# Expert results scattered to rows of token and choice, tokens gathered in quarter rows ahead and turned on VectorE

## The chip, the cores and the metric

The kernel runs on one core of a Trainium2 chip. The metric is the device time of one execution in microseconds. The kernel before took 2192.16 us, the median of 3 runs (2192.0 to 2193.31 us).

## What is computed

A decoder layer on 1024 tokens of width 1024: a token mixer (a state space model, a gated unit and a cross attention, merged and projected), then a mixture of experts, then a norm. The mixer is not touched by the change. Of the experts this matters:

```
g_idx = argmax(xf @ w_group + b_group)              # one of 8 groups
top_vals, top_loc = top_k(logits of the group's 8 experts, 2)
weights = group probability * softmax(top_vals)     # 2 choices per token
per expert e:  y = (silu(xb @ w1[e]) * (xb @ w3[e])) @ w2[e]
h = h + sum over the 2 choices of weight * y;  out = rmsnorm(h, g_final)
```

There are 64 experts. w1 and w3 are 1024x512 and w2 is 512x1024, all float32, so an expert's weights are 6.29 MB and all of them 403 MB. The 2048 pairs of token and choice are spread unevenly. With the given inputs the reference's routing gives 39 experts of at most 32 tokens, 17 of 33 to 64, 6 of 65 to 96, one of 105 and one of 130.

## The kernel before, in words

All five engines' programs are written out by hand, with semaphores between them. The order is: the mixer; an output stage over 8 tiles of 128 tokens, which also makes the norm of each tile, its router logits and its places in a table of tokens by expert; the expert stage; a last stage over 8 tiles that sums, norms and stores.

**The expert stage.** A unit is up to 32 tokens (`CAP`) of one expert; here there are 100 units. The 64 experts are put in an order that alternates light and heavy ones (`place_col`, L1792 to L1804) and take turns in four slots of SBUF (`SLOTS`), one set of weights each. Every engine runs the same two loops, `each_unit` (L403): over the experts, where it loads three numbers (first unit of the slot, end, shift) from `spans` into registers (L409 to L411), and inside over the units of the expert.

- SyncE (`refill`, L568): when the last unit of the slot's old expert has done its up products, it issues the new expert's token list (L575) and w1 and w3 (L520), and after its down products w2 (L524).
- GpSimd (`gather`, L711): waits until the last gather has landed, copies the unit's column of the list to `gather_idx` (L714), waits until TensorE has turned the last unit's tokens, and issues one indirect DMA of 32 rows of 4 KB into `xg` (L719). `xg` is one buffer.
- TensorE (`work`, L1090): 64 up products from `xT` into a PSUM bank (L1100), the transpose of the hidden rows, then `turn_tokens` (L1083): 8 transposes of the next unit's tokens (both L779), then 32 down products (L1114).
- VectorE: gate times up (L1846), copy of the transposed hidden (L1848), copy of the turned tokens to `xT` (L1841).
- ScalarE (L1319): silu (L1321); then it waits for the stores of the slot's last unit, copies the unit's result to `y_rows` (L1325) and issues four direct DMAs of 32 KB (L1328) to `y_dram`, rows in the order of units.

```
pool.wait_ge(tok_gathered, u * 16 + 16)
nc.gpsimd.tensor_copy(gather_idx[:, :], idx).then_inc(idx_copied, 1)
pool.wait_ge(tok_turned, u + 1)
pool.indirect_dma_start(xg, None, xf_dram, ... gather_idx ...)
```

**The last stage.** After the last stores GpSimd gathers, for each tile of 128 tokens, the rows of both choices from `y_dram` (`pick`, L739, L749), 16 indirect DMAs of 512 KB, into four pairs of buffers (`PICKS`). TensorE sums the even tiles (L772), VectorE the odd ones (L1405, L1879); ScalarE squares, VectorE norms, SyncE stores (L595). The rows of `y_dram` that stand in no unit are cleared early in the mixer by four DMAs of 2 MB (L633).

Of the kernel before, what the change touches and what calls it, by code (L numbers as in the profile page):

```python
# [25 lines left out]
I32 = mybir.dt.int32  # L26
# [32 lines left out]
PICKS = 4  # L59
UNITS = E + 2 * T // CAP  # L60
SLOT_UNITS = TURNS + 2 * T // CAP
# [45 lines left out]
def program(nc, x, mem, g_mix, g_mem, w_in, w_gate, b_gate, lam_re, lam_im, log_dt, b_re, b_im,  # L107
# [3 lines left out]
    with ctx:  # L111
# [37 lines left out]
        token_id = sb("token_id", [P, NT], I32)  # L149
        no_token = sb("no_token", [CAP, 1], I32)  # L150
        table_row = sb("table_row", [P, 2, NT], I32)
        y_row = sb("y_row", [P, 2, NT], I32)
# [3 lines left out]
        spans = sb("spans", [1, 5, E], I32)  # L156
        by_expert = sb("by_expert", [E, 12])
        tokens = sb("tokens", [CAP, SLOTS, COLS], I32)
        gather_idx = sb("gather_idx", [CAP, 1], I32)
# [41 lines left out]
        def tiles(n, k):  # L201
# [28 lines left out]
        pick_rows = unit[9][:, 0:2 * NT * E].rearrange("p (i c e) -> p i c e", i=NT, c=2)  # L230
# [4 lines left out]
        n_units, all_ends = (late[:, 144 + E * n:144 + E * (n + 1)] for n in range(2))  # L235
        pos, base = (late[:, 400 + 16 * n:416 + 16 * n].rearrange("p (i c) -> p i c", i=NT) for n in range(2))
        gsum, den = late[:, 432:440], late[:, 440:448]
        row_of = late[:, 448:464].rearrange("p (i c) -> p i c", i=NT)
# [12 lines left out]
        in_order = now[0:1, 0:5 * E].rearrange("p (n e) -> p n e", n=5)  # L251
# [12 lines left out]
        xg = gain_b[0:CAP, :]  # L264
        xT = gain_a[:, 0:256].rearrange("p (k t) -> p k t", k=KD)
# [5 lines left out]

        y_pick = [[mid_store[:, D * (2 * b + c):D * (2 * b + c + 1)] for c in range(2)] for b in range(PICKS)]
        mix_out = [pair[5][:, D * b:D * (b + 1)] for b in range(PICKS)]
        square_out = pair[5][:, D * PICKS:D * (PICKS + 1)]
        choice_diag = pair[5][:, D * PICKS + D:D * PICKS + 2 * D].rearrange("p (i c t) -> p i c t", i=NT // 2, c=2)
# [6 lines left out]
        table_dram = nc.dram_tensor("expert_token_table", [E * T, 1], I32, kind="Internal").ap()  # L282
        table_of = table_dram.rearrange("(e p n) a -> e p (n a)", e=E, p=CAP)
        y_dram = nc.dram_tensor("unit_results", [UNITS * CAP, D], F32, kind="Internal").ap()
# [7 lines left out]
        x_root, x_row_loaded = sem("x_root"), [sem(f"x_row{i}_loaded") for i in range(NT)]  # L292
# [7 lines left out]
        h_loaded = [sem(f"h_loaded{i}") for i in range(NT)]  # L300
        spatial_loaded, spatial_masked = sem("spatial_loaded"), sem("spatial_masked")
        idx_copied = sem("idx_copied")
        tok_gathered, tok_turned, xT_ready = sem("tok_gathered"), sem("tok_turned"), sem("xT_ready")
# [7 lines left out]
        toep_cleared, results_cleared = sem("toep_cleared"), sem("results_cleared")  # L311
# [6 lines left out]
        table_blank, tile_routed, rows_picked, weighted = (  # L318
            sem("table_blank"), sem("tile_routed"), sem("rows_picked"), sem("weighted"))
        tokens_loaded = [sem(f"tokens_loaded{s}") for s in range(SLOTS)]  # L320
        units_known, order_known = sem("units_known"), sem("order_known")
# [7 lines left out]
        picked = [sem(f"picked{b}") for b in range(PICKS)]  # L329
# [3 lines left out]
        out_stored = [sem(f"out_stored{b}") for b in range(PICKS)]  # L333
# [6 lines left out]
        for family, rows in (  # L340
# [8 lines left out]
                        ("branches", 6 * KD), ("out", 4 * NT), ("order", 2))),  # L349
# [53 lines left out]
        def each_unit(eng, body, enter=None, shift_row=2, less=0):  # L403


            with eng.Fori(0, TURNS) as t:
                for s in range(SLOTS):
                    at = bass.ds(t * SLOTS + s, 1)
                    first = eng.value_load(spans[0:1, 0, at], min_val=0, max_val=SLOT_UNITS)  # L409
                    end = eng.value_load(spans[0:1, 1, at], min_val=0, max_val=SLOT_UNITS)  # L410
                    shift = eng.value_load(spans[0:1, shift_row, at], min_val=0, max_val=2 * UNITS)  # L411
                    if enter:
                        enter(s, t)
                    with eng.Fori(first, end) as c:
                        u = nc.s_assert_within(c + shift - less if less else c + shift, 0, UNITS - 1, skip_runtime_bounds_check_because=(
                            "the units of all experts are at most UNITS"))
                        body(c, s, u, t, first)
# [5 lines left out]
        def _(sp):  # L423
# [4 lines left out]
            for i in range(NT):  # L428
                if i == 4:
                    sp.dma_start(w_v, columns(w_in[0], 2 * W, W)).then_inc(w_loaded["v"], 16)  # L430
                sp.dma_start(x_rows[i], x_tiles[i]).then_inc(x_row_loaded[i], 16)
# [31 lines left out]
            sp.wait_ge(results_cleared, 16 * 4)  # L463
# [72 lines left out]
            sp.dma_start(w_route[:, :, 0:NG], w_group[0].rearrange("(p k) n -> p k n", p=P)  # L536
                         ).then_inc(w_loaded["route"], 16)
            sp.dma_start(w_route[:, :, NG:], w_router[0].rearrange("(p k) n -> p k n", p=P)
# [27 lines left out]
            sp.wait_ge(rows_picked, 1)  # L566
            expert_up(up, 3, halves=(1,))

            def refill(e, s):
                first = sp.value_load(spans[0:1, 0, bass.ds(e, 1)], min_val=0, max_val=SLOT_UNITS)  # L570
                chosen_expert = sp.value_load(spans[0:1, 4, bass.ds(e, 1)], min_val=0, max_val=E - 1)
# [3 lines left out]
                sp.dma_start(tokens[:, s], table_of[bass.ds(chosen_expert, 1)].rearrange("e p n -> (e p) n")  # L575
                             ).then_inc(tokens_loaded[s], 16)
# [19 lines left out]
            for b in range(PICKS):  # L596
                sp.wait_ge(out_stored[b], 16 * NT // PICKS)
# [1308 lines left out]
```

## Time and profile before

| | |
|---|---|
| runs, us | 2192.16, 2193.31, 2192.0 |
| profiled execution, own time | 2188.43 us |
| its span | 2186.3 us |
| mean granted TensorE clock | 0.924 |
| TensorE busy | 1819.5 us, 83% |
| VectorE, ScalarE, GpSimd busy | 22%, 12%, 11% |
| moved by DMA | 510.97 MB |

The profiled execution is 3.7 us shorter than the median of the runs. The span runs from the first to the last instruction. In the profile PE is TensorE, PEld its weight loads, DVE VectorE, ACT ScalarE, POOL GpSimd and SP SyncE; ACTq, POOLq and SPq are the instruction streams of those engines, where register work, waits and the issuing of DMAs stand. L1100 is a line of the kernel before. The DMA share is how busy the core's 16 DMA engines are on average; it can read slightly above 1. The expert stage runs from about 1110 to 2134 us.

### The profile page before, as it was taken

The page shows a single profiled execution, that of the slowest core. Times are in us where ns is not written, and L with a number is a line of the kernel's source. Part 1 is how long each engine was busy: PE and PEld are TensorE (multiplying, and loading weights), DVE is VectorE, ACT ScalarE, POOL GpSimd, SP SyncE. Part 2 cuts the span into 40 slices and gives each one's busy share as a digit, 9 for nine tenths or more (in the row PEclk, how much of TensorE's full clock was granted, in tenths as well). Part 3 has the DMA queues.
Part 4 walks back from the last instruction along what each step waited for, and adds up shares of the span by engine and source line. Part 5 has one row for each costly group of instructions (what it writes and reads, how often), then busy time and mean ns, then how long its engine had stood idle before and what let it go on. Part 6 is the DMA issues. An engine that isn't in the chain of part 4 may idle for free.

```text
span 2186.3 us, 39333 instructions
## 1 busy us (share of the span) xinstructions
PE 1819.5 (83%) x13926; PEld 994.2 (45%) x13927; DVE 477.7 (22%) x1147; ACT 252.1 (12%) x543; POOL 245.0 (11%) x375
## 2 busy tenths in 40 slices
PE   7999999999999999999757567777777777676774
PEld 3676456644444444445534234444444444443442
DVE  5618214511110111146510000011011010001015
ACT  4012314200000000011100000000000000000002
POOL 1951000000000000001111011011111111111112
PEclk9999999999999999999779788899899888888898
DMA  6320321201111110073669999898999999999996
GB/s 194 145 61 22 128 77 34 68 2 43 43 43 43 43 43 38 0 288 122 250 265 419 419 413 401 346 406 339 407 401 403 405 401 410 408 399 407 410 365 237
DMA packets 152792, 510.97 MB, mean 234 GB/s; under 512 B 34400, under 2 KB 84064, under 8 KB 135840
## 3 DMA queue, kind: packets, MB, share of 16 engines
q1 hardware_dynamic: 122096, 461.36, 54.5%
q0 software_dynamic: 8816, 27.02, 3.5%
q10 hardware_dynamic: 21840, 22.06, 2.9%
q8 instruction: 24, 0.39, 0.1%
q14 instruction: 16, 0.13, 0.0%
HBM read 479.84 MB, written 34.35 MB: 235 GB/s over the span
## 4 chain that ended last, share of the span: by engine, by line
PE 59%; DMA 17%; ACTq 7%; SPq 5%; issue 4%; DVE 3%; ACT 2%; POOLq 0%; POOL 0%; DVEq 0%
PE act_bank L772 27%; PE dve_bank L772 15%; DMA unit_results<-lane_row 6%; PE act_bank L1114 5%; DMA unit_results<-spatialT 4%; ACTq L1328 4%; DMA gain_b<-xf_rows,gather_idx 4%; PE dve_bank L779 4%; PE act_bank L1100 3%; SPq L575 3%; SPq L520 2%; PE dve_bank L1114 2%; DMA tokens<-expert_token_table 1%; SPq L524 1%; ACTq L410 1%
## 5 line engine op out<-in xcount | busy, mean ns | idle before, releaser
L772 PE MATMUL act_bank<-norm_store,unit 128*128 128x512 f32 x1024 | 449.8, 592 | 0.2 <-DMA unit<-in_w_in 0.2
L772 PEld LDWEIGHTS act_bank<-norm_store,unit 128*128 128x128 f32 x1024 | 194.0, 190 | 239.4 <-issue 238.4
L1100 PE MATMUL act_bank<-unit,gain_a 128*32 128x256 f32 x3200 | 186.9, 385 | 24.5 <-issue 23.9
L1114 PE MATMUL act_bank<-unit,gain_a 128*32 128x256 f32 x2432 | 202.9, 490 | 0.0
L1846 DVE TENSOR_TENSOR gain_a<-gain_a,act_bank 128x128 f32<-128x128 f32 x100 | 28.8, 288 | 773.0 <-ACT gain_a L1321 765.0
L779 PE MATMUL dve_bank<-ident,gain_a 128*128 128x128 f32 x100 | 35.2, 352 | 169.2 <-DVE gain_a L1846 167.2
L1100 PEld LDWEIGHTS act_bank<-unit,gain_a 128*32 128x32 f32 x3200 | 109.3, 112 | 105.3 <-issue 49.8
L779 PE MATMUL dve_bank<-ident,gain_b 32*128 32x32 f32 x808 | 78.2, 242 | 77.4 <-DMA gain_b<-xf_rows,gather_idx 77.3
L1681 DVE TENSOR_TENSOR rows_store<-dve_bank,rows_store 128x512 f32<-128x512 f32 x48 | 33.3, 693 | 431.0 <-PE dve_bank L772 431.0
L1114 PEld LDWEIGHTS act_bank<-unit,gain_a 128*32 128x32 f32 x2432 | 95.1, 135 | 63.8 <-issue 42.5
L719 POOL DMA_INDIRECT gain_b<-xf_rows,gather_idx x101 | 94.3, 934 | 248.3 <-PE dve_bank L779 240.0
L772 PE MATMUL dve_bank<-unit,unit 128*128 128x512 f32 x256 | 115.1, 592 | 0.0
L772 PE MATMUL dve_bank<-unit,mid_store 128*128 128x512 f32 x256 | 111.4, 594 | 2.4 <-DVE mid_store L1685 2.4
L779 PEld LDWEIGHTS dve_bank<-ident,gain_a 128*128 128x128 f32 x100 | 14.6, 146 | 217.2 <-DVE gain_a L1846 214.3
L772 PE MATMUL act_bank<-unit,norm_store 128*128 128x512 f32 x256 | 112.3, 599 | 0.0
L1100 PE MATMUL act_bank<-norm_store,gain_a 128*32 128x256 f32 x1536 | 95.2, 403 | 19.2 <-issue 19.2
L779 PEld LDWEIGHTS dve_bank<-ident,gain_b 32*128 32x128 f32 x808 | 67.4, 158 | 92.8 <-issue 86.7
L1100 PE MATMUL act_bank<-mid_store,gain_a 128*32 128x256 f32 x1664 | 100.7, 395 | 9.3 <-issue 9.0
L772 PE MATMUL dve_bank<-unit 128*128 128x512 f32 (+1 forms) x320 | 104.0, 474 | 2.6 <-ACT unit L1156 1.7
L714 POOL COPY gather_idx<-tokens 32x1 int32 x100 | 17.7, 177 | 670.6 <-DMA gain_b<-xf_rows,gather_idx 558.4
L772 PEld LDWEIGHTS act_bank<-unit,norm_store 128*128 128x128 f32 x256 | 64.6, 254 | 44.5 <-issue 30.0
L1100 PEld LDWEIGHTS act_bank<-mid_store,gain_a 128*32 128x32 f32 x1664 | 57.1, 115 | 55.8 <-issue 27.8
(268 smaller groups left out, 1507.8 us busy)
## 6 DMA issues: line engine op xcount, KB each, us to landing
unit<-in_w SPq DMA_DIRECT2D x112, 2048.0 KB
norm_store<-in_w SPq DMA_DIRECT2D x32, 2048.0 KB
mid_store<-in_w SPq DMA_DIRECT2D x32, 2048.0 KB
rows_store<-in_w SPq DMA_DIRECT2D x16, 2048.0 KB
unit<-in_w_gate SPq DMA_DIRECT2D x24, 512.0 KB, 5.2
unit<-in_w_in SPq DMA_DIRECT2D x4, 2048.0 KB, 8.7
unit_results<-unit POOLq DMA_DIRECT2D x4, 2048.0 KB, 13.4
unit_results<-lane_row ACTq DMA_DIRECT2D x200, 32.0 KB
```

Source lines behind the costliest of these rows:

```text
L410: end = eng.value_load(spans[0:1, 1, at], min_val=0, max_val=SLOT_UNITS)
L520: sp.dma_start(w13[s][:, z].rearrange("p k n -> p (k n)"), w_up[z].rearrange("e (p k) n -> p (e k n)", p=P)).then_inc(up_loaded[s], 16)
L524: sp.dma_start(w2s[s], w_down.rearrange("e (k p) n -> p (e k) n", p=P)).then_inc(down_loaded[s], 16)
L575: sp.dma_start(tokens[:, s], table_of[bass.ds(chosen_expert, 1)].rearrange("e p n -> (e p) n")).then_inc(tokens_loaded[s], 16)
L719: pool.indirect_dma_start(xg, None, xf_dram, bass.IndirectOffsetOnAxis(ap=gather_idx[:, 0:1], axis=0), bounds_check=T - 1, oob_is_err=Fals ...
L772: ins = nc.tensor.matmul(out_, stationary, moving, start=first and n == 0, stop=n == len(pairs) - 1)
L779: ins = nc.tensor.transpose(bank[:, n * rows:(n + 1) * rows], block_, ident[0:rows, 0:rows])
L1100: ins = nc.tensor.matmul(act_bank[0][h * CAP:(h + 1) * CAP, 0:2 * FQ].rearrange("t (w n) -> t w n", w=2), xT[:, k], w13[s][:, :, k, h * FQ ...
L1114: ins = nc.tensor.matmul(y_bank[s][z * CAP:(z + 1) * CAP, 0:DQ], hidT[:, j], w2s[s][:, j, z * DQ:(z + 1) * DQ], start=j == 0, stop=j == QU ...
L1328: act.dma_start(y_dram[bass.ds(u * CAP, CAP), z * DQ:(z + 1) * DQ], y_rows[s][z * CAP:(z + 1) * CAP]).then_inc(per_slot["y_stored"][s], 16)
L1681: v.tensor_tensor(parts[i], dve_bank[b % 4][:, :], gates[n % 4], ALU.mult).then_inc(dve_drained, 1)
L1846: v.tensor_tensor(hid, silu_g, act_bank[0][:, FQ:2 * FQ], ALU.mult).then_inc(per_slot["hid_ready"][s], 1)
```

## The change

- **Table.** An entry of the token table now holds two float32 numbers: four times the token's number (its first quarter row in `xf_rows`), and four times (2 x token + choice), its first quarter row in the results. An empty entry holds 16384, out of range for both.
- **Gathers.** A token's row is fetched as four quarter rows of 1 KB, quarter q to partitions 32q to 32q+31, so a gather has 128 rows. Each list is loaded four times, one for each quarter, by ScalarE, three experts ahead (`list_ahead`, 4 DMAs); GpSimd adds 0 to 3 to it (`tensor_scalar`). There are four buffers of tokens in place of one: `open_rows` (the first unit of an expert) and `next_rows` (the following units), two of each. GpSimd fills them two experts ahead; inside an expert it fetches the unit after the next. An expert thus has two gathers more than it has units; those past its last token fetch nothing.
- **Turning.** VectorE turns a unit's tokens with one 32x32 block transpose of 128x256 (`v.transpose`), once after each unit and once more at the end of an expert. TensorE's token transposes are gone.
- **Results.** ScalarE's four stores of a unit are replaced by one scatter from GpSimd: a copy of the unit's result rows to `y_idx`, then an indirect DMA of 128 quarter rows, the empty ones dropped. The rows are in the order of token and choice, so the last stage reads each tile by one direct DMA of 1 MB from SyncE into eight buffers; the 16 picks, their row numbers (L1824 to L1829), and the clearing of `y_dram` are gone.
- **Small.** The router weights are loaded in another row order and the norm is written straight; one TensorE product of the ordering is gone.

```diff
-            def gather(idx, u):
-                pool.wait_ge(tok_gathered, u * 16 + 16)
...
+            def open_expert(s, t):
+
+                f = s % 2
+                pool.wait_ge(tokens_loaded[s], t * (16 * QUARTERS) + 16 * QUARTERS)
                 pool.nop(nofuse=True)
...
+                nc.gpsimd.tensor_scalar(tokens[:, s, 0:COLS], token_lists[:, s, 0:COLS], quarter_no[:, 0:1], None,
+                                        ALU.add).then_inc(list_made[f], 1)
+                pool.wait_ge(list_made[f], t * 2 + (s // 2 + 1))
+                gather(open_rows[f], tokens[:, s, 0, 0:1], open_landed[f])
+
+            def open_next(s):
+                gather(next_rows[s % 2], tokens[:, s, 1, 0:1], next_landed[s])
+
+            def scatter(c, s, first):
...
+                pool.wait_ge(per_slot["y_drained"][s], c + 2)
+                nc.gpsimd.tensor_copy(y_idx[:, s:s + 1], tokens[:, s, bass.ds(column, 1), 1]).then_inc(y_indexed[s], 1)
+                pool.wait_ge(y_indexed[s], c + 2)
+                pool.indirect_dma_start(y_dram, bass.IndirectOffsetOnAxis(ap=y_idx[:, s:s + 1], axis=0), y_rows[s],
+                                        None, bounds_check=2 * T * QUARTERS - 1, oob_is_err=False
+                                        ).then_inc(per_slot["y_stored"][s], 16)
+
+            def unit_work(c, s, u, t, first):
...
+                pool.wait_ge(xT_ready, turns_at(u, s, t) + 1)
+                nc.gpsimd.tensor_copy(next_idx[:, f:f + 1], tokens[:, s, bass.ds(column, 1), 0]
+                                      ).then_inc(next_indexed[s], 1)
+                pool.wait_ge(next_indexed[s], c + 1)
+                gather(next_rows[f], next_idx[:, f:f + 1], next_landed[s])
+                scatter(c, s, first)
...
+            def enter(s, t, u):
+                pool.wait_ge(xT_ready, turns_at(u, s, t))
+                open_expert(*ahead(s, t))
+
+            def leave(s, t, end, units):
+                pool.wait_ge(next_landed[s], (end + t) * 16 + 16)
+                open_next(ahead(s, t)[0])
...
-                for z in range(QUARTERS):
-                    act.dma_start(y_dram[bass.ds(u * CAP, CAP), z * DQ:(z + 1) * DQ],
-                                  y_rows[s][z * CAP:(z + 1) * CAP]).then_inc(per_slot["y_stored"][s], 16)
...
+            def list_ahead(s, t, u):
+                at, slot = t * SLOTS + s + LISTS, (s + LISTS) % SLOTS
+                used = act.value_load(spans[0:1, 0, bass.ds(at, 1)], min_val=0, max_val=SLOT_UNITS)
+                chosen_expert = act.value_load(spans[0:1, 2, bass.ds(at, 1)], min_val=0, max_val=E - 1)
+                act.wait_ge(y_indexed[slot], used + 1)
+                load_list(slot, table_of[bass.ds(chosen_expert, 1)].rearrange("e p n -> (e p) n"))
...
+            def turn_tokens(rows):
+                v.transpose(xT, rows.rearrange("p (m k) -> p k m", k=KD)).then_inc(xT_ready, 1)
...
+                sp.dma_start(y_both[i], y_tiles[i]).then_inc(row_loaded[i], 16)
```

**GpSimd in the expert stage.** Before, one unit of the expert in slot 0 and the way to the next expert (L714 the copy of the column, L719 the gather into `gain_b`, which holds `xg`; L409 the first of the register loads):

```order
L414 UNCONDITIONAL_BRANCH [waits tokens_loaded0]
L414 ISA
L714 ISA [waits tok_gathered]
L714 COPY gather_idx<-tokens 32x1
L715 REGISTER_ALU
L719 DMA gain_b<-xf_rows,gather_idx 32x1024 [waits idx_copied,tok_turned]
L414 REGISTER_ALU
L414 COMPARE_AND_BRANCH
L409 ISA
L409 TENSOR_LOAD spans
```

Now one unit of the expert in slot 1 and the gather at its end (L734 is a gather into a token buffer in `gain_b`, `gain_a` holds the lists, `choice_results` is the results' tensor, `lane_row` a result buffer). The register loads (L418 to L420) follow, and ahead of a unit, at an expert's entry, stand L742, the `tensor_scalar` on the list of the expert two ahead, and its gather:

```order
L770 ISA [waits xT_ready]
L770 COPY next_idx<-gain_a 128x1
L772 REGISTER_ALU
L734 DMA gain_b<-xf_rows,next_idx 128x256 [waits next_indexed1]
L754 REGISTER_ALU
L756 ISA [waits y_drained1]
L756 COPY y_idx<-gain_a 128x1
L759 DMA choice_results<-lane_row,y_idx 8192x256 [waits y_indexed1]
L423 REGISTER_ALU
L423 COMPARE_AND_BRANCH
L786 ISA
L734 DMA gain_b<-xf_rows,gain_a 128x256 [waits next_landed1]
```

What was one copy and one indirect DMA for a unit is now two of each, and every expert adds a `tensor_scalar` and two gathers. The last row waits for the landing of the gather that was issued in the expert's last unit (the fourth row), and stands ahead of the next expert's register loads.

**ScalarE at the end of a unit and the start of the next expert.** Before (L1325 copies the result, L1328 stores a quarter of it):

```order
L1325 ACTIVATE lane_row<-act_bank 128x256 [waits y_stored0]
L1326 REGISTER_ALU
L1328 ISA [waits y_drained0]
L1328 DMA unit_results<-lane_row 32x256
L1328 ISA
L1328 DMA unit_results<-lane_row 32x256
```

Now, between the result's copy (L1356, after which nothing is stored) with the three register loads and the next expert's silu (L1352), stands this:

```order
L1361 TENSOR_LOAD spans
L1361 ISA x2
L1362 REGISTER_ALU
L1338 ISA [waits y_indexed0]
L1338 DMA gain_a<-expert_token_table 32x64 x4
L423 UNCONDITIONAL_BRANCH
L423 ISA
L1352 ACTIVATE gain_a<-act_bank 128x128 [waits gu_ready1]
```

The four stores after the copy have left ScalarE; two register loads, a wait for GpSimd's index copy of the expert before, and four list loads have come in ahead of the next expert's silu.

## Rows read from the trace of the kernel before

**Rows 1.** Busy time by stretch: us, engines' busy (instructions), granted clock, DMA share, GB/s.

```profile
1395.00:1412.00 17.00, 11.61 (x157) 5.98 (x149) 1.17 (x4) 1.32 (x4) 1.29 (x3) 0.80 0.66 251
1480.00:1490.00 10.00, 9.27 (x133) 5.09 (x137) 1.43 (x4) 0.66 (x2) 1.67 (x3) 0.83 0.28 62
...
1117.00:2118.00 1001.00, 722.46 (x10234) 414.21 (x10238) 98.08 (x293) 64.04 (x194) 108.69 (x195) 0.87 1.00 399
```

**Rows 2.** The page's DMA issues: times, KB each.

```profile
unit_results<-lane_row ACTq DMA_DIRECT2D x200, 32.0 KB
```

**Rows 3.** Waits from 1110 to 2134 us: total us, times, longest.

```profile
ACT lane_row L1325 <- DMA unit_results<-lane_row: 120.6, 15, 9.2
...
ACT spatialT L1325 <- DMA unit_results<-spatialT: 89.4, 11, 9.1
```

**Rows 4.** Timeline, ScalarE around a two-unit expert: start, us, what.

```profile
1604.67 0.28 ACT L1321 ACTIVATE gain_a<-act_bank 128x128 f32<-128x128 f32 x1 [4.20 <-PE act_bank L1100]
1608.58 0.38 ACT L1325 ACTIVATE spatialT<-act_bank 128x256 f32<-128x256 f32 x1 [3.64 <-PE act_bank L1114]
1609.16 1.76 ACTq L1328 DMA_DIRECT2D unit_results<-spatialT  x4
...
1618.79 0.38 ACT L1325 ACTIVATE spatialT<-act_bank 128x256 f32<-128x256 f32 x1 [6.85 <-DMA unit_results<-spatialT]
```

**Rows 5.** Chain of waits at the stage's start, GpSimd's stream: start, us.

```profile
1095.04 0.07 POOLq L406
...
1097.47 0.06 POOLq L414
...
1098.45 0.55 issue
1099.00 0.03 POOLq L414
...
1099.22 7.65 DMA gain_b<-xf_rows,gather_idx
```

**Rows 6.** Timeline, GpSimd: a copy and gather that wait for nothing else.

```profile
1328.81 0.18 POOL L714 COPY gather_idx<-tokens 32x1 int32 x1 [11.46 <-DMA tokens<-expert_token_table]
1329.84 0.94 POOL L719 DMA_INDIRECT gain_b<-xf_rows,gather_idx  x1 [0.85 <-POOL gather_idx L714]
```

**Rows 7.** All 101 gathers of L719, issue to landing.

```profile
DMA to landing us min/median/max: 2.8/7.0/7.9
```

**Rows 8.** Three single gathers: one row, then two with no row in range.

```profile
L719 POOL DMA_INDIRECT gain_b<-xf_rows,gather_idx x1: 933/933/933, 2036.7 to 2036.7; - x1
...
DMA to landing us min/median/max: 6.4/6.4/6.4
...
L719 POOL DMA_INDIRECT gain_b<-xf_rows,gather_idx x1: 934/934/934, 2124.3 to 2124.3; - x1
...
DMA to landing us min/median/max: 5.0/5.0/5.0
...
L701 POOL DMA_INDIRECT gain_b<-in_x,no_token x1: 982/982/982, 928.9 to 928.9; - x1
...
DMA to landing us min/median/max: 4.8/4.8/4.8
```

**Rows 9.** Stretches beside two of these gathers, columns as in Rows 1.

```profile
930.00:934.00 4.00, 4.00 (x11) 1.85 (x10) 0.00 (x0) 0.00 (x0) 0.00 (x0) 1.00 1.21 329
...
2124.00:2129.00 5.00, 3.65 (x72) 2.02 (x68) 0.00 (x0) 0.38 (x1) 0.93 (x1) 1.00 0.59 225
```

**Rows 10.** Timeline: the first up products.

```profile
1109.98 5.96 PE L1100 MATMUL act_bank<-norm_store,gain_a 128*32 128x256 f32 x64 [1.95 <-issue]
```

**Rows 11.** Timeline: the last result copied, the first pick, the last tile's sum.

```profile
2134.09 0.38 ACT L1325 ACTIVATE spatialT<-dve_bank 128x256 f32<-128x256 f32 x1 [3.35 <-PE dve_bank L1114]
...
2138.37 0.97 POOL L749 DMA_INDIRECT mid_store<-unit_results,y_row  x1 [13.10 <-DMA unit_results<-spatialT]
...
2172.10 1.28 DVE L1405 SCALAR_TENSOR_TENSOR norm_store<-mid_store,choice_w,norm_store 128x1024 f32<-128x1024 f32 x1 [1.80 <-DMA mid_store<-unit_results,y_row]
```

More of the change, by code:

```diff
@@ L291, in program @@
         x_loaded = [sem(f"x_loaded{s}") for s in range(2)]
-        x_root, x_row_loaded = sem("x_root"), [sem(f"x_row{i}_loaded") for i in range(NT)]
+        x_root, row_loaded = sem("x_root"), [sem(f"row{i}_loaded") for i in range(NT)]
         root_made = [sem(f"root_made{s}") for s in range(2)]
@@ L332, in program @@
         out_made = [sem(f"out_made{z}") for z in range(2)]
-        out_stored = [sem(f"out_stored{b}") for b in range(PICKS)]
+        out_stored = [sem(f"out_stored{b}") for b in range(OUTS)]
         act_jobs, dve_jobs = {}, {}
@@ L628, in _ @@
             pool.wait_ge(toep_cleared, 1)
-            for z in range(2):
-                rows = (E + z * (UNITS - E) // 2) * CAP
-                for n in range(2):
-                    a = rows + n * 4 * P
-                    pool.dma_start(y_dram[a:a + 4 * P].rearrange("(p b) d -> p (b d)", p=P), unit[6][:, :]
-                                   ).then_inc(results_cleared, 16)
             def double_phases(have):
@@ L733, in _ @@
-            units = (pool.value_load(spans[0:1, 1, E - 1:E], min_val=0, max_val=SLOT_UNITS)
-                     + pool.value_load(spans[0:1, 2, E - 1:E], min_val=0, max_val=UNITS))
-            gather(no_token[:, :], units)
-            last = [pool.value_load(spans[0:1, 1, e:e + 1], min_val=0, max_val=SLOT_UNITS) for e in last_of]
-            for s in range(SLOTS):
-                pool.wait_ge(per_slot["y_stored"][s], last[s] * (16 * QUARTERS) + 16 * QUARTERS)
-            pool.nop(nofuse=True)
@@ new lines, in ahead @@
+            def ahead(s, t):
+                return (s + AHEAD) % SLOTS, t + (s + AHEAD) // SLOTS
+            def enter(s, t, u):
+                pool.wait_ge(xT_ready, turns_at(u, s, t))
+                pool.nop(nofuse=True)
+                open_expert(*ahead(s, t))
+            def leave(s, t, end, units):
+                pool.wait_ge(next_landed[s], (end + t) * 16 + 16)
+                pool.nop(nofuse=True)
+                open_next(ahead(s, t)[0])
+            for s in range(AHEAD):
+                open_expert(s, 0)
+                open_next(s)
@@ L757, in _ @@
+            each_unit(pool, unit_work, enter, leave)
+            ends = [pool.value_load(spans[0:1, 0, E + s:E + s + 1], min_val=0, max_val=SLOT_UNITS) for s in range(AHEAD)]
+            for s in range(AHEAD):
+                pool.wait_ge(open_landed[s], 16 * (E // 2 + 1))
+                pool.wait_ge(next_landed[s], ends[s] * 16 + 16 * (TURNS + 1))
         @block.tensor
@@ L1069, in _ @@
             rank(NT - 1)
-            pe.wait_ge(units_known, 1)
+            pe.wait_ge(order_known, 1)
             bank = dve_bank_for(job(dve_jobs, "order"))
-            nc.tensor.matmul(bank[0:E, 0:1], lower[0:E, 0:E], of_expert[:, 0:1], start=True, stop=True
-                             ).then_inc(dve_filled, 1)
-            pe.wait_ge(order_known, 1)
-            bank = dve_bank_for(job(dve_jobs, "order", 1))
-            for n in range(3):
+            for n in (0, 2):
                 ins = nc.tensor.matmul(bank[0:1, n * E:(n + 1) * E], of_expert[:, n:n + 1], placed, start=True, stop=True)
@@ L1308, in _, with load_list @@
             act.wait_ge(table_filled, 16 * 2 * NT)
-            for s in range(SLOTS):
-                act.dma_start(tokens[:, s], table_of[s]).then_inc(tokens_loaded[s], 16)
+            def load_list(s, rows):
+                for q in range(QUARTERS):
+                    act.dma_start(token_lists[q * CAP:(q + 1) * CAP, s, 0:COLS].rearrange("p n a -> p (n a)"), rows
+                                  ).then_inc(tokens_loaded[s], 16)
+            for s in range(LISTS):
+                load_list(s, table_of[s])
             act.wait_ge(routed, 1)
```

279 lines of the change are left out of this document (138 added, 141 removed).

## The prediction

> **What bounds the kernel now.** First the busy time by stretch. From 1117 us, when the first refill is under way, to 2118 us the 16 DMA engines show a share of 1.00 on average at 399 GB/s, with two dips, about 1400 us (0.66 over 17 us) and 1480 us (0.28 over 10 us) [rows 1]. Idle DMA time in them is 0.34 x 17 + 0.72 x 10 = 13.0 us. So the stage is bound by fetching 403 MB of weights, and an expert (6.29 MB) costs about 16 us of DMA time. Then the waits: they show a second chain that is almost as long. ScalarE waited 120.6 + 89.4 = 210 us for the stores of a unit's result before it could copy the next one of the same slot [rows 3]. The timeline shows how: a result copied at 1608.58 is stored by four DMAs, and the next is copied only at 1618.79, after 6.85 us of waiting [rows 4]. The same silu at 1604.67 was 3.9 us ahead of its result [rows 4]. The reader is to see that the weights set the pace, while the chain through the small DMAs only just keeps up: what the change does to either can decide.
>
> **What goes, on the path.** (1) The start. Now the first gather lands at 1106.87 (1099.22 + 7.65) [rows 5], and the first up products start at 1109.98 [rows 10]: 3.1 us of TensorE transposes, a copy and waits. One VectorE transpose takes their place. No row has one; it is at least 0.3 us, as the nearest VectorE operation, and hardly more than 1 us. I take 0.45 us with 0.2 us of waking: 2.4 us earlier, so about 1107.6. (2) The two dips: 13.0 us at most, if the chain gets faster. (3) The last stage. The first pick starts at 2138.37 and the last tile's sum at 2172.10, 14.2 us ahead of the end [rows 11]. Eight direct loads of 1 MB move 8.39 MB, 21.0 us at 399 GB/s; with 2.4 us until the first bytes count (2.8 is the least landing of a gather [rows 7], 0.4 less for a direct load), the last sum starts 23.4 us after the last result has landed, and the end comes at 37.6 us instead of 47.9 us (2186.3 - 2138.4): 10.3 us less. (4) The clearing of the results (four DMAs in the mixer) was waited for by a copy on SyncE that TensorE needs much later; I cost it at nothing, hidden by TensorE's matmuls, which never wait there. The norm in straight order and the router weights in small pieces lie beside TensorE's other matmuls of a tile: nothing. (5) TensorE's token transposes, under 1 us per unit, lie on the chain, not on the DMA.
>
> **What comes.** DMA traffic: results shrink from 3200 to 2048 rows of 4 KB (now in 400 stores, half of them under this name [rows 2]), 4.7 MB or 11.8 us at 399 GB/s. Against it, gathers come in four times as many pieces, and the lists are four times as many and twice as large. No row prices pieces of 256 B or 1 KB apart from the rest; between the whole 11.8 us gained and as much lost, I take 0.
>
> **GpSimd is the term that decides.** Its stream is followed step by step. A copy and a gather behind it take 1.03 us from start to start [rows 6]; an indirect DMA keeps the engine 0.94 us [rows 6], but its stream goes on 0.2 us before that starts (1099.00 against 1099.22) and needs 0.55 us to hand it over [rows 5]. The register loads of an expert take 2.4 us (1095.04 to 1097.47) [rows 5]. So for an expert of one unit, from the start of the unit's gather: L us until it has landed, 0.75 to the start of the next gather, from 0.2 before that 2.4 for the loads, 0.25 for the `tensor_scalar` (nearest row: the copy, 0.18 [rows 6]), 0.85 to the opening gather, 0.95 for it, 1.03 to the next unit's gather: L + 6.0, with 0.1 for the added waits L + 6.1. The scatter (2 us) fits inside L.
>
> L is the landing of a gather that brings nothing. All gathers took 2.8 to 7.9 us, 7.0 in the median [rows 7]. The gather at 2036.7 brings, by the routing, one row and took 6.4 us; two with no row in range took 5.0 and 4.8 us [rows 8], the one beside a DMA share of 0.59, the other while the queue was just filling [rows 9]. So L lies between 4.8 and 6.4 under full load; I take 5.7, midway between 5.0 and 6.4, since both neighbours are imperfect in opposite ways. The round is 11.8 us.
>
> A further unit of the same expert costs the store's way round: 1.7 us from the result's copy to the scatter (copy 0.4, wake 0.25, 1.03 [rows 4, 6]) and its landing. As a full gather it would take 7.3 (between the median and the longest [rows 7]), together 9.0; at worst, as the four stores do today, about 10.7. I take 9.0, since it is one DMA.
>
> 64 x 11.8 + 36 x 9.0 = 755 + 324 = 1079 us. The weights alone need 1024 (first up products to last result, 1110 to 2134.1) - 13.0 = 1011 us. GpSimd is thus longer, the DMA idles 6.5% of the time, and in those times gathers and scatters land 2.9 and 4.5 us sooner: 64 x 2.9 x 0.065 + 36 x 4.5 x 0.065 = 22 us less, 1057. The first gather of this kind starts 7 us after the first up products, the last result is copied 1.4 us after the last such gather, and one round less counts: 1107.6 + 7 + 1057 - 11.8 + 1.4 = 2161, against 2134.1: **+27 us**. The last result lands 5.1 us after its copy begins (0.4, 1.3 and a landing of 3.4, DMA nearly idle) against 4.3 (2134.09 to 2138.37 [rows 11]): +0.8.
>
> ScalarE: silu to result 3.9, copy 0.4, loads 2.4, two more 1.1, four list DMAs 1.8 (four stores take 1.76 [rows 4]): 9.6 us per expert, below GpSimd's 11.8. It is not the bound, and TensorE, which waits for its silu, follows.
>
> **Sum**, against the profiled execution of 2188.4 us: + 27 + 0.8 - 10.3 = 2205.9; it stands 3.7 us under the median of the runs, so **2209.6 us**.
>
> **A rule against the rows.** The trace has gathers landing after 7.0 us in the median. The Trainium skill (DMA: Bandwidth & Descriptors, Anatomy of one DMA) gives an indirect or direct GpSimd DMA 2.0 us plus its bytes at 436 GB/s. By it L would be 2.0 us and a scatter 2.3 us, so an estimate from it is 64 x 8.1 + 36 x 4.0 = 662 us: GpSimd would not bound, and rival A would come true. The trace does not agree: only the least of 101 landings, 2.8 us, comes near it.
> The Trainium skill (SBUF — State Buffer, SBUF: two separate sides) also says that some VectorE operations lock GpSimd out while it writes descriptors, which speaks against turning on VectorE; if the transposes did so, each would hold up an indirect DMA. The rows of L719 here, 0.93 and 0.94 us, show no such stall, but none of them stands beside a transpose.
>
> **Rivals.** *A, faster: the weights stay the bound.* If L is 4.8 and steps overlap a little more, GpSimd's sum is 64 x 10.9 + 324 = 1022, less its own relief, no longer than the weights' 1011. Then the dips go too: 2188.4 - 2.4 - 13.0 + 0.8 - 10.3 + 3.7 = 2167 us; 2180 if the dips stay. For it: GpSimd is busy 11% now, and every gather is early. Against it: the blocking wait at each expert's end. It decides where L + 6.1 falls under about 10.8.
> *B, much slower: landings as long as the worst rows.* L = 6.4, scatters 10.7 from their start, so 12.4 per further unit: 64 x 12.5 + 36 x 12.4 = 1246, relief by 19% idle DMA 98: 1148; last result 2252, total about 2300 us. For it: four DMAs per round now share GpSimd's queue. Against it: the queue carries one packet run per engine, not four stores.
> *C, no change:* the gain of the last stage and start just pays for GpSimd: 2192 us. It needs a last result at about 2144.
> *D, the change does not do what it says:* the gathers were hidden already (the result stores are the longer wait [rows 3]), so fetching two experts ahead gains nothing; it is inside A and C.
>
> **How the numbers follow.** A measurement of this kernel can tell about 0.2%, 4.4 us, from no change. My case (GpSimd longer than the weights, 2197 to 2245) has 0.42, B's end beyond it 0.08, C 0.07, A 0.43. The range leaves out 1 in 10 at either end: low is A with the traffic's 11.8 us gained, 2155, and 3 us more for the steps costed at nothing, 2152; high lies between my case and B, 2258. Both signs hold most of the chance, so: the likeliest case's own range is 2197 to 2245 us.
>
> **What would show it.** Right: DMA share in the stage about 0.93 or with many dips; GpSimd's gather at the expert's end held by the landing before it, in nearly every round; rounds of about 12 us between one-unit experts late in the stage; the gathers' median near 6 us; the first up products near 1107.6; 38 us from the last landing to the end. Wrong: a DMA share of 1.0 to the end with GpSimd waiting for results (rival A), or scatters landing after 9 us or more (B), or a transpose above 1.5 us.

## The result and the profile after

| | before | after |
|---|---|---|
| median of 4 runs, us | 2192.08 | 2246.56 |
| ratio after to before, 95% interval | | 1.0253 (1.0227 to 1.0279) |
| profiled execution, own time | 2188.43 | 2242.68 |
| span | 2186.3 | 2240.8 |
| first up products | 1109.98 | 1108.57 |
| last result copied | 2134.09 | 2196.05 |
| from there to the span's end | 52.2 | 44.75 |

The change is slower by 54.5 us. The span splits it without a rest: the start is 1.4 us earlier, the expert stage 63.4 us longer (1087.5 against 1024.1), the end 7.5 us shorter. The forecast was slower by 17.5 us, with 2197 to 2245 us as its range; 2246.6 lies 1.6 us above it. Direction (0.50 for slower against 0.43 for faster) and mechanism came as forecast, the size of the stage's term did not.

From the page of the changed kernel, the DMA share in 40 slices and the queues:

```profile
DMA  6021321110011111352799998979889999898975
...
q1 hardware_dynamic: 120368, 469.50, 53.8%
q0 software_dynamic: 17248, 19.28, 2.6%
q10 hardware_dynamic: 15312, 11.13, 1.5%
```

The expert stage is the stretch of 9s, 8s and 7s from the 21st slice. Busy time by stretch, columns as in Rows 1, shows how much is missing:

```profile
1117.00:2165.00 1048.00, 669.84 (x9267) 361.38 (x9263) 148.25 (x345) 63.26 (x191) 390.90 (x563) 0.86 0.95 380
```

The share is 0.95 and 380 GB/s, where [rows 1] had 1.00 and 399. The DMA waits for somebody. The waits from 1110 to 2190 us tell for whom (us in all, times, longest):

```profile
DVE gain_a L1871 <- ACT gain_a L1352: 747.6, 99, 11.8
...
POOL gain_b L734 <- DMA gain_b<-xf_rows,next_idx: 244.2, 59, 5.4
...
DVE gain_a L1867 <- DMA gain_b<-xf_rows,next_idx: 124.2, 26, 8.5
ACT lane_row L1356 <- DMA choice_results<-lane_row,y_idx: 119.5, 14, 13.2
POOL next_idx L770 <- DVE gain_a L1867: 111.0, 38, 4.9
...
ACT spatialT L1356 <- DMA choice_results<-spatialT,y_idx: 109.1, 14, 11.7
```

The largest wait (VectorE for the silu) is that of an engine that is busy 14% of this time and comes behind TensorE and ScalarE in every unit. The telling one is GpSimd's: at 59 of the 64 expert ends its stream stands still for the landing of a gather, 4.1 us each. It is the wait that the order of instructions had shown. ScalarE still waits for results to land, 228.6 us in 28 waits, where [rows 3] had 210 in 26. GpSimd's timeline over a round of one unit, from the copy of the unit's row numbers (L770) to the next such copy:

```profile
1914.76 0.20 POOL L770 COPY next_idx<-gain_a 128x1 int32 x1
1915.78 1.05 POOL L734 DMA_INDIRECT gain_b<-xf_rows,next_idx  x1 [0.82 <-ACT spatialT L1356]
1916.83 0.19 POOL L756 COPY y_idx<-gain_a 128x1 int32 x1
1917.88 1.03 POOL L759 DMA_INDIRECT choice_results<-spatialT,y_idx  x1 [0.85 <-POOL y_idx L756]
1923.33 1.05 POOL L734 DMA_INDIRECT gain_b<-xf_rows,gain_a  x1 [4.42 <-DMA gain_b<-xf_rows,next_idx]
1925.30 0.45 POOL L742 TENSOR_SCALAR gain_a<-gain_a,quarter_no 128x64 int32<-128x64 f32 x1 [0.92 <-issue]
1926.56 1.08 POOL L734 DMA_INDIRECT gain_b<-xf_rows,gain_a  x1 [0.82 <-POOL gain_a L742]
1927.64 0.20 POOL L770 COPY next_idx<-gain_a 128x1 int32 x1
```

The round is 12.88 us: 1.02 to the empty gather, 7.55 until the next gather may start behind its landing, 1.97 with the register loads, 1.26, 1.08. Over the stage the 38 rounds of one unit between such copies have a mean of 13.1 us, the 17 of two units 20.3, the 6 of three 26.7. The scatter (1917.88) stands inside the wait, as forecast.

The chain of waits from 1900 to 1935 us has the same wait in it. Here the landing stands alone, without the 0.75 us from it to the start of the next gather:

```profile
1915.78 6.75 DMA gain_b<-xf_rows,next_idx
```

It is an empty gather (the round has one unit), and it landed after 6.75 us. The forecast had taken 5.7.

### The profile page after: what moved, and what is told of

It reads as the page before. It is cut to its first block, busy times and chain, and to the rows that moved or that the text cites. A ratio compares the mean times of both kernels' runs of the same rounds, so it can differ in the third digit from the quotient of the medians.

```text
span 2240.8 us, 38700 instructions
## 1 busy us (share of the span) xinstructions
PE 1779.7 (79%) x13114; PEld 949.4 (42%) x13115; DVE 524.9 (23%) x1205; ACT 252.4 (11%) x543; POOL 535.6 (24%) x760
## 4 chain that ended last, share of the span: by engine, by line
PE 51%; DMA 24%; issue 10%; POOLq 5%; DVE 3%; POOL 3%; ACTq 1%; ACT 1%; DVEq 0%
PE act_bank L815 27%; DMA gain_b<-xf_rows,next_idx 21%; PE dve_bank L815 14%; PE act_bank L1130 3%; POOLq L419 1%; POOLq L420 1%; PE act_bank L1143 1%; POOL gain_a L742 1%; PE dve_bank L822 1%; POOLq L418 1%; DVE gain_a L1867 1%; PE act_bank L822 1%; POOL gain_b L734 1%; DMA choice_results<-spatialT,y_idx 1%; POOL next_idx L770 1%
## 5 line engine op out<-in xcount | busy, mean ns | idle before, releaser
L1130 PE MATMUL act_bank<-unit,gain_a 128*32 128x256 f32 x3200 | 215.0, 427 | 78.7 <-DVE gain_a L1867 60.2
L1143 PE MATMUL act_bank<-unit,gain_a 128*32 128x256 f32 x2432 | 189.0, 463 | 43.8 <-DVE gain_a L1873 43.8
L734 POOL DMA_INDIRECT gain_b<-xf_rows,gain_a x132 | 139.6, 1058 | 301.1 <-DMA gain_b<-xf_rows,next_idx 244.2
L1130 PEld LDWEIGHTS act_bank<-unit,gain_a 128*32 128x32 f32 x3200 | 117.1, 124 | 180.8 <-issue 136.0
L1130 PE MATMUL act_bank<-norm_store,gain_a 128*32 128x256 f32 x1536 | 102.7, 426 | 52.2 <-DVE gain_a L1867 35.6
L1143 PEld LDWEIGHTS act_bank<-unit,gain_a 128*32 128x32 f32 x2432 | 98.9, 128 | 103.7 <-issue 85.1
L1867 DVE STREAM_TRANSPOSE gain_a<-gain_b 128x256 f32<-128x256 f32 x165 | 105.5, 639 | 140.6 <-DMA gain_b<-xf_rows,next_idx 124.2
L734 POOL DMA_INDIRECT gain_b<-xf_rows,next_idx x100 | 105.3, 1053 | 85.3 <-POOL next_idx L770 74.8
L815 PE MATMUL dve_bank<-unit,unit 128*128 128x512 f32 x272 | 122.6, 592 | 0.0
L1130 PEld LDWEIGHTS act_bank<-norm_store,gain_a 128*32 128x32 f32 x1536 | 56.2, 123 | 99.6 <-issue 78.0
## 6 DMA issues: line engine op xcount, KB each, us to landing
norm_store<-in_w SPq DMA_DIRECT2D x32, 2048.0 KB, 17.5
```

Of the source, the lines that this page charges most:

```text
L734: pool.indirect_dma_start(rows, None, xf_quarters, bass.IndirectOffsetOnAxis(ap=idx, axis=0), bounds_check=T * QUARTERS - 1, oob_is_err=Fa ...
L815: ins = nc.tensor.matmul(out_, stationary, moving, start=first and n == 0, stop=n == len(pairs) - 1)
L1130: ins = nc.tensor.matmul(act_bank[0][h * CAP:(h + 1) * CAP, 0:2 * FQ].rearrange("t (w n) -> t w n", w=2), xT[:, k], w13[s][:, :, k, h * FQ ...
L1143: ins = nc.tensor.matmul(y_bank[s][z * CAP:(z + 1) * CAP, 0:DQ], hidT[:, j], w2s[s][:, j, z * DQ:(z + 1) * DQ], start=j == 0, stop=j == QU ...
L1867: v.transpose(xT, rows.rearrange("p (m k) -> p k m", k=KD)).then_inc(xT_ready, 1)
```

## The experiments

Nine kernels ran. Times are medians; the kernel before had 2189.2, 2189.9 and 2191.1 us beside them in the three series. The intervals are those of the ratios; differences between two runs of the table are taken from the medians. Two kernels leave something out or change the result: e3_rows32 fetches only a quarter of the tokens of an expert's further units, and e9_store_flat lays the results' quarter rows down in another order.

| run | edit to | us | ratio to before (95%) |
|---|---|---|---|
| e1_four_buffers | the change | 2141.95 | 0.9784 (0.9767 to 0.9800) |
| e2_no_empty | the change | 2145.82 | 0.9791 (0.9772 to 0.9810) |
| e3_rows32 | the change | 2199.82 | 1.0047 (1.0030 to 1.0064) |
| e4_one_more | the change | 2284.89 | 1.0439 (1.0422 to 1.0457) |
| e5_short_lists | the change | 2239.79 | 1.0217 (1.0176 to 1.0259) |
| e6_one_list | e1 | 2181.18 | 0.9959 (0.9941 to 0.9977) |
| e7_spare_on_e2 | e2 | 2150.11 | 0.9820 (0.9783 to 0.9856) |
| e8_before_one_store | before | 2321.37 | 1.0605 (1.0564 to 1.0647) |
| e9_store_flat | before | 2181.03 | 0.9948 (0.9930 to 0.9967) |

**The wait taken away, and its control.** With four `next_rows` buffers the gather for the expert after next goes to a buffer that nobody is filling.

```diff
         next_rows = [gain_b[:, 512 * f + 256:512 * f + 512] for f in range(2)]
+        next_rows += [more_rows[:, :], gain_a[:, 768:1024]]
...
-                pool.wait_ge(next_landed[s], (end + t) * 16 + 16)
+                pool.wait_ge(next_landed[(s - 1) % SLOTS], (end_before + t) * 16 + 16)
```

> Four next_rows buffers, one for each slot, in place of two; GpSimd's gather at an expert's end then waits for the landing of the gather of the expert before, which is a round old. (The lists hold 14 columns in place of 32, to make room.) Theory G (GpSimd's round, held by the blocking wait, sets the stage): the round was 13.1 us with 7.57 us from the empty gather's start to the next gather; without the wait its stream needs about 9 us, so the weights are the bound again. The last result comes 62 to 75 us earlier: 2171 to 2185 us. Rival P (the small pieces of gathers, scatters and lists slow the weights' DMA): the wait only moves, 2240 us or more. Rival I (GpSimd's own instructions, four indirect DMAs where there was one, are too slow even without the wait): between, 2200 to 2235 us.

The control keeps the shorter lists and has the old wait:

> The control for the four-buffer run: the change with lists of 14 columns in place of 32 (the room for the two buffers), and still two next_rows buffers and the wait. If the buffers were what gave the 105 us there, this run stays at 2240 to 2250 us. Rival: shorter lists (8 KB to 3.5 KB a load, a shorter tensor_scalar) give a part: 0.1 us of each round, 6 us, or up to 20 us if the lists' DMAs were a load on the queues.

Measured: 2141.95 and 2239.79 us. The two buffers give 97.8 us. The shorter lists give at most the other 6.8 of the 104.6, which the noise can hide (1.0217 with 1.0176 to 1.0259, against 1.0253 with 1.0227 to 1.0279). Theory G stands, I and P fall, and the result is 29 us below the range that G had given: the kernel with four buffers is 47 us faster than before. Its busy time by stretch and its waits from 1110 to 2094 us:

```profile
1110.00:2000.00 890.00, 593.16 (x8863) 331.16 (x8855) 142.38 (x330) 60.23 (x182) 365.21 (x536) 0.91 1.00 408
```

```profile
POOL next_idx L778 <- DVE gain_a L1884: 234.3, 78, 8.0
...
ACT lane_row L1373 <- DMA choice_results<-lane_row,y_idx: 96.9, 18, 7.1
...
ACT spatialT L1373 <- DMA choice_results<-spatialT,y_idx: 81.8, 16, 7.4
```

The share is 1.00 at 408 GB/s. GpSimd now waits 78 times for VectorE's transposes. With the DMA share at 1.00 that is a wait for the pace of the weights. In no line of this view does it wait for its own gather any more.

**The cause taken away in another way.** Here the last unit of an expert fetches nothing and turns nothing after it.

```diff
-                    with eng.Fori(first, end) as c:
-                        body(c, s, c + shift, t, first)
...
+                        with eng.If(end > first + 1):
+                            with eng.Fori(first, end - 1) as c:
+                                body(c, s, c + shift, t, first)
+                        last(s, t, end, first)
...
```

> The last unit of an expert fetches nothing and VectorE turns nothing after it (the loops of GpSimd and VectorE run to the unit before the last, the last unit stands behind them, with a branch around the loop). Per expert one copy, one gather and one transpose less, and the wait at its end is for a gather that is a round old. Theory G: the weights bound the stage, as in the four-buffer run, 2168 to 2185 us. Rival P (pieces): 64 gathers of 128 descriptors that bring nothing are gone, which may give back part, but 2225 us or more. Rival A (ScalarE's list loads and its longer way between units are the next bound): 2190 to 2215 us.

Measured 2145.82 us, again below G's range, by 22 us. The first edit keeps the empty gathers and waits for an older one, the second has no empty gathers; in both the wait for a fresh gather is gone, and they end within 4 us of each other. Then the same load on GpSimd was added to the change and to this kernel:

```diff
                 open_next(ahead(s, t)[0])
+                pool.wait_ge(spare_landed, (t * SLOTS + s) * 16 + 16)
...
+                gather(spare[:, :], no_token[:, 0:1], spare_landed)
```

> One more empty gather for each expert, behind the gather at the expert's end, outside the wait; nothing else. Theory G: every round longer by the 1.05 us that an indirect DMA takes on GpSimd, 64 x 1.05 = 67 us: 2300 to 2320 us. Rival P (DMA bound): 128 descriptors more per expert against 6.3 MB, so at most 10 us: 2245 to 2257 us.

> The kernel without empty gathers (2145.8 us) with one more empty gather for each expert, the same edit that cost the change 38 us. Theory W (GpSimd is no longer the bound): 2144 to 2150 us. Rival (GpSimd still sets the pace): 38 us or more, 2184 us.

In the change it cost 38.3 us (2284.89), in the kernel without empty gathers 4.3 us (2150.11, where the runs without it went from 2139.5 to 2150.5). So GpSimd is the bound in the one and not in the other. But 2284.89 us is below G's 2300 and above P's 2257: the 38.3 us are 0.60 per expert, not 1.05. GpSimd's timeline in that run shows why:

```profile
1918.25 1.04 POOL L736 DMA_INDIRECT gain_b<-xf_rows,gain_a  x1 [4.48 <-DMA gain_b<-xf_rows,next_idx]
1919.60 1.00 POOL L736 DMA_INDIRECT spare<-xf_rows,no_token  x1 [0.31 <-issue]
1920.90 0.45 POOL L744 TENSOR_SCALAR gain_a<-gain_a,quarter_no 128x64 int32<-128x64 f32 x1 [0.30 <-issue]
```

From the gather at the expert's end to the `tensor_scalar` it is 2.65 us with the extra gather between them and 1.97 without (1923.33 to 1925.30 above); over 63 ends the means are 2.78 and 2.12. The stream works through the register loads there, from 1918.8 to 1920.6 us in the chain of this run, and the extra DMA's engine time lies partly beside them.

**Where the landing comes from.** The gathers into `next_rows` get 32 indices in place of 128:

```diff
...
-                gather(next_rows[f], next_idx[:, f:f + 1], next_landed[s])
+                gather(next_rows[f][0:CAP], next_idx[0:CAP, f:f + 1], next_landed[s])
```

> The gathers into next_rows have 32 indices in place of 128 (three quarters of the tokens of an expert's second and later units are left out; all else is as in the change). Theory Q (an empty gather's landing under load is queueing and does not depend on its indices): still 6.5 to 7 us from issue to landing at the expert's end, 2240 to 2250 us. Rival N (128 indices are what made the landing longer than the 5.7 us forecast): landing 5.7 us or less, 64 x 1.1 = 70 us less, 2176 to 2200 us.

Measured 2199.82 us, 46.7 less than the change. From the timeline, one such wait:

```profile
1914.57 0.94 POOL L734 DMA_INDIRECT gain_b<-xf_rows,next_idx  x1 [0.82 <-POOL next_idx L770]
...
1921.06 0.92 POOL L734 DMA_INDIRECT gain_b<-xf_rows,gain_a  x1 [3.03 <-DMA gain_b<-xf_rows,next_idx]
```

From start to start it is 6.49 us here, in the mean of 58 such pairs 6.76, where the change has 7.57 in 59. So 0.81 us of an empty gather's landing is due to 96 indices more, though they bring nothing, and 64 x 0.81 = 52 us is about what the run gave. The time lies at the upper end of rival N's range, and theory Q falls: the indices are the greater part of what was missing. What is left, 6.76 - 0.75 = 6.0 us for 32 indices, is close to the 5.7 of the forecast.

**Small DMAs.** With the weights as the bound again, what do the small queues cost? One list DMA in place of four, on the four-buffer kernel (both calls shortened):

```diff
-                for q in range(QUARTERS):
-                    act.dma_start(token_lists[q * CAP:(q + 1) * CAP, s, 0:HELD]..., rows[:, 0:2 * HELD])
+                act.dma_start(token_lists[:, s, 0:HELD]..., bc(rows[:, 0:2 * HELD], 0, QUARTERS))
```

> The four-buffer kernel (2141.95 us) with one DMA for a token list in place of four, its source read four times (and a wait for the stored rows ahead of the first gather, which is long satisfied). Theory W (with GpSimd's wait gone the weights bound the stage, and each 1% of DMA time of the small queues costs 1% of it): ScalarE's queue has 0.9% of the stage's 987 us, of which two thirds may go: 4 to 7 us less, 2135 to 2138 us. Rival (the small DMAs cost nothing beside the weights): 2140 to 2144 us.

Measured 2181.18 us: 39 us slower than with four, a miss for both. And on the kernel before, one result store in place of four:

```diff
-                for z in range(QUARTERS):
-                    act.dma_start(y_dram[bass.ds(u * CAP, CAP), z * DQ:(z + 1) * DQ],
-                                  y_rows[s][z * CAP:(z + 1) * CAP]).then_inc(per_slot["y_stored"][s], 16)
+                act.dma_start(y_dram[bass.ds(u * CAP, CAP)].rearrange("r (z d) -> z r d", z=QUARTERS),
+                              y_rows[s]).then_inc(per_slot["y_stored"][s], 16)
```

> The kernel before (2189 us in these runs) with a unit's result stored by one DMA of 128 rows in place of four of 32. Theory W (before, the weights were the bound but for 13 us of dips that the stores' way round made, and small DMAs cost their share): the dips go and a part of the 4% of ScalarE's queue, 2168 to 2178 us. Rival (the dips have another cause, and the number of DMAs does not matter): 2186 to 2191 us.

Measured 2321.37 us: 132 us slower, again outside both. The waits of ScalarE from 1110 to 2264 us:

```profile
ACT spatialT L1325 <- DMA unit_results<-spatialT: 214.7, 14, 23.5
...
ACT lane_row L1325 <- DMA unit_results<-lane_row: 174.4, 12, 20.2
```

They go up to 23.5 us, where [rows 3] had 9.2. In the list's run GpSimd waited 163.2 us for lists, against 30.3 us in the four-buffer kernel (both lines are of the waits in the stage):

```profile
POOL gain_a L752 <- DMA gain_a<-expert_token_table: 163.2, 35, 7.7
```

```profile
POOL gain_a L750 <- DMA gain_a<-expert_token_table: 30.3, 23, 2.4
```

Both edits had made one DMA whose slowest dimension has 4 entries. The next run, on the kernel before, keeps the single store and its 128 pieces of 1 KB, and lays them down in one dimension of 128 (the lines in which it differs from the last edit):

```diff
-                act.dma_start(y_dram[bass.ds(u * CAP, CAP)].rearrange("r (z d) -> z r d", z=QUARTERS),
+                act.dma_start(y_dram[bass.ds(u * CAP, CAP)].rearrange("r (z d) -> (r z) d", z=QUARTERS),
```

> The kernel before with a unit's result stored by one DMA, as in the run that took 2321 us, but its 128 quarter rows one behind the other in the stored order of lanes (one dimension of 128 rows of 1 KB in place of 4 by 32). The results' quarter rows thus stand in another order, so the output is another; the bytes, the rows and the picks are the same. Theory S (the 4 by 32 shape is what made the single store slow, its rows being spread over fewer DMA engines): its landing falls under that of the four stores, the dips go: 2165 to 2185 us. Rival (any single DMA of 128 rows lands as late under load): 2300 us or more.

Measured 2181.03 us, 140 us less than with 4 by 32. The pieces' places in memory differ too: they lie one behind the other here, and 4 KB apart with 4 by 32. But the four stores of before also write theirs 4 KB apart, and take 2191 us beside this run, so the distance is not what cost 130 us; the shape is what is left. Landing of these stores, from the line's own view:

```profile
DMA to landing us min/median/max: 5.5/9.5/10.4
```

For the four stores of before no view gives this line. In a stretch with the same experts, the first row of each pair below is the issue and the second the next copy of the slot, which waits for the landing; before, then with the single flat store:

```profile
1385.71 1.75 ACTq L1328 DMA_DIRECT2D unit_results<-lane_row  x4
1397.37 0.38 ACT L1325 ACTIVATE lane_row<-act_bank 128x256 f32<-128x256 f32 x1 [9.12 <-DMA unit_results<-lane_row]
```

```profile
1386.10 0.37 ACTq L1327 DMA_DIRECT2D unit_results<-lane_row  x1
1394.94 0.38 ACT L1325 ACTIVATE lane_row<-act_bank 128x256 f32<-128x256 f32 x1 [7.86 <-DMA unit_results<-lane_row]
```

It is 11.7 us before and 8.8 now (10.2 for the store ahead of it, where before had 11.7). Of the difference 1.4 us are the issues of three more stores. ScalarE's waits for these stores fall from 210 us in 26 [rows 3] to 144.6 in 22, and the two dips of [rows 1] are gone:

```profile
ACT lane_row L1325 <- DMA unit_results<-lane_row: 87.0, 13, 9.2
...
ACT spatialT L1325 <- DMA unit_results<-spatialT: 57.6, 9, 8.2
```

```profile
1395.00:1412.00 17.00, 12.84 (x158) 6.80 (x150) 2.01 (x6) 1.28 (x5) 2.22 (x4) 0.80 0.98 387
1480.00:1490.00 10.00, 7.94 (x140) 4.95 (x133) 1.00 (x3) 0.66 (x2) 2.05 (x3) 1.00 0.97 404
```

So theory S holds in both points: the landing fell under that of the four stores, and the dips went. The stage (1114.30 to 2123.91 us) takes 14.5 us less than before's 1024.1, and the run 0.52% less. The 13.0 us that the prediction had put on the dips were there to be had. The Trainium skill (DMA: Bandwidth & Descriptors, Why a DMA increments its semaphore by 16 and not by 1) says that a DMA runs on the largest number of engines, up to 16, that divides the slowest dimensions of both its sides. An estimate by it is 4 engines for 4 by 32, and 16 for 32 or 128 rows. The two runs agree with it in time; no view here shows the engines of one DMA.

## Why the prediction was wrong in size

- **The start**, forecast 2.4 us earlier: 1.4. The VectorE transpose takes 0.64 us, not 0.45. The first gather starts 5.6 us later than before (1104.79), since its list comes later, and lands after 2.90 us in place of 7.65 [rows 5]. The forecast had neither; that they nearly cancel is luck. Small, right sign.
- **GpSimd's round for an expert**, "L + 6.1, 11.8 us": 13.1 us. This is the step that failed: L, the landing of a gather that brings nothing, was put too low. L was set at 5.7, midway between a one-row gather under load (6.4) and an empty one beside a light load (5.0) [rows 8, 9]. It measured 6.75 to 6.8 in the change. Both neighbours had 32 indices, and 0.8 us is what 96 more cost, which no row of before could show. The rest of the round, 6.1, was forecast to 0.2 us. The term: 64 x 1.3 = 83 us more than forecast, of which L has about 70.
- **A further unit**, 9.0 us on the scatter's way round: 7.1 (from 13.1, 20.3 and 26.7 us for one, two and three units). The way round that was priced, from the result's copy through the scatter to the next copy, is not the one that sets the pace. ScalarE does wait for a scatter 28 times, but in the page's chain the gathers into `next_rows` have 21% of the span and the scatters from `spatialT` 1%: behind a further unit, too, it is mostly the next gather that is waited for. 36 x 1.9 = 68 us less than forecast. The two errors nearly cancel, and that is luck.
- **The relief**, 22 us less because the DMA idles at times: not seen. The share is 0.95, and yet of the 59 waits at the expert ends the shortest is 6.15 us from start to start and the mean 7.57. The landings shorten only when no weights are left to load (from 2176 us on). The means above are measured ones, so what relief there was is in them already. With it the balance closes: 83 - 68 + 22 = 37 us, against 35 us that the last result came later than forecast (62.0 against 27).
- **The DMA traffic**, taken as 0 between 11.8 gained and lost: in the four-buffer kernel it lies at the gaining end. Queues from 1110 to 2134 us of before, and from 1107 to 2094 us of the four-buffer kernel (packets, MB, share of 16 engines):

```profile
q1 hardware_dynamic: 53127, 382.44, 92.4%
q10 hardware_dynamic: 19008, 13.00, 4.0%
q0 software_dynamic: 4800, 8.27, 2.6%
```

```profile
q1 hardware_dynamic: 50086, 381.61, 94.0%
q0 software_dynamic: 15675, 16.88, 5.0%
q10 hardware_dynamic: 12144, 0.92, 0.9%
```

  The small queues took 6.6% of 1024 us, 68 us, and now 5.9% of 987, 58 us: 10 us less, in spite of three times the packets on GpSimd's queue. The weights' own queue went from 946 us to 928 for the same bytes, 404 to 411 GB/s. Its cause stays open; with the single flat store the weights' queue of before had 403 GB/s (381.98 MB in 93.8% of 1010 us).
- **The last stage**, forecast 9.5 us shorter in all: 7.5. The results landed about 4 us after their copy, a little sooner than the 5.1 forecast, but behind them VectorE and not the eight loads set the pace. VectorE's timeline has no wait in its rows from 2218 us to the end. The rows below are the norms of the first two tiles and the two sums of the third of the four odd tiles:

```profile
2218.87 1.41 DVE L1398 SCALAR_TENSOR_TENSOR unit<-act_bank,rstd,unit 128x512 f32<-128x512 f32 x2
2220.19 1.28 DVE L1398 SCALAR_TENSOR_TENSOR unit<-norm_store,rstd,unit 128x1024 f32<-128x1024 f32 x1
2221.39 1.28 DVE L1440 SCALAR_TENSOR_TENSOR norm_store<-unit,choice_w,norm_store 128x1024 f32<-128x1024 f32 x1
2222.70 1.28 DVE L1912 SCALAR_TENSOR_TENSOR norm_store<-unit,choice_w,norm_store 128x1024 f32<-128x1024 f32 x1
```

- **The rivals.** A had its condition right, that GpSimd must fall below the weights, but the change as it stands never met it. With the wait gone it comes true, and at 2142 us it is 25 us under A's 2167: the stage takes 987 us, not 1011. By the queues above it is 37 us shorter than before's 1024: about 9 us of idle DMA time (1% of 1024, now 0.1%), 10 of the small queues, 18 of the weights' rate. B was nearer in L (6.4) and wrong about a further unit (12.4 against 7.1), and its total of 2300 us is further off than 2209.6. D stays open: before lost its dips by a single store alone, without fetching ahead, and no run tells what fetching ahead gains by itself.
- **The Trainium skill's 2.0 us** (DMA: Bandwidth & Descriptors, Anatomy of one DMA): a gather by that rule would have let A come true. The landing of 6.75 us, median 6.7 over the gathers of L734, does not agree with it under this load. The lock between VectorE and GpSimd (the Trainium skill, SBUF — State Buffer, SBUF: two separate sides) that the prediction weighed did not show in the length of these DMAs. Of the indirect DMAs of L734 from `gain_a` in the stage, 21 run beside a transpose and take 1.04 us in the median, the 105 others 1.07; one of them:

```profile
1690.11 1.42 DVE L1867 STREAM_TRANSPOSE gain_a<-gain_b 128x256 f32<-128x256 f32 x2
...
1690.33 1.03 POOL L734 DMA_INDIRECT gain_b<-xf_rows,gain_a  x1 [4.20 <-DMA gain_b<-xf_rows,next_idx]
```

  Against 0.94 us of before [rows 8], the 1.05 us of the change are the price of 128 indices: with 32 it is 0.94 us again, in the run above.

## What to carry to other kernels

A wait is as dear as what stands behind it in its stream. Here an empty gather, fetched for nobody, was waited for at the one place where GpSimd had the next expert's whole work still ahead; 2 KB of SBUF per partition, or a loop that stops one unit earlier, turned a change that lost 2.5% into one that gains 2.1 to 2.2%. Price a wait on a DMA with rows of the same number of indices and under full load, and look before merging small DMAs at the slowest dimension that the merged one has.

## What the hardware showed that was not expected

- An indirect DMA with all indices out of range lands nearly as late under load as one that brings rows: 6.75 us against the median of 7.0 over all gathers of before [rows 7], most of which bring rows. 96 more such indices cost 0.8 us in landing and 0.1 us on GpSimd's engine.
- A store of 128 KB in a shape of 4 by 32 rows cost the kernel 140 us over the same bytes in one dimension of 128 rows, 1.4 us for each of 100 units; a list load of the same kind cost 39 us over four of 32 rows each. For the list no other shape was run, so there the shape as the cause is argued and not shown.
- GpSimd's stream runs ahead of its indirect DMAs, so that an extra one of 1.0 us lengthened the way to the next instruction by 0.66 us.
